# An eighth place for the experts' weights, and eight low parts of weights subtracted on GpSimd

## The chip, the cores and the metric

One core of a Trainium2 chip runs the whole program. The metric is the device time of one execution in microseconds; three runs of the kernel before gave 1318.97, 1319.60 and 1320.26 us (median 1319.6). Every time within an execution is counted from the first instruction of its profile.

## What is computed

Two transformer blocks in f32 over 256 tokens of width 1024. The first block ends in a mixture of experts; the second has a long convolution (Hyena), a differential attention and a gated feed-forward part. Cut to what the change touches:

```python
def hierarchical_moe(xn, w_rg, b_rg, w_re, b_re, w1, w3, w2):      # 4 groups of 8 experts, 2 experts for each token
    ...
    def block_ffn(args):
        tok, e = args
        xb = xt[tok]
        hb = jax.nn.silu(xb @ w1[e]) * (xb @ w3[e])                # w1, w3: 1024 x 512; w2: 512 x 1024
        return hb @ w2[e]
    ...
# first block: x += hybrid_mixer(...); x += memory_cross_attention(...); x += hierarchical_moe(...); rmsnorm(x, norm_f_g)
# second block: h = modulate(rmsnorm_2(x, g_mix_pre)); proj = h @ w_in     (columns: Hyena 3 x 512, q, k, v 512 each, gates 2048)
    y_hy = hyena_branch(proj[..., :OFF_Q], *hy_p) @ w_hy_up
    ...
    o = diff_attention(q, k_all, v_all, lam)                       # keys and values of x and of the context
    y_att = heads_out(o, subln_g, lam_init) @ w_att_up
    g_hy, g_att = split(sigmoid(proj[..., OFF_G:]))
    mixed = (g_hy * y_hy + g_att * y_att) @ w_out
    x = x + g1 * rmsnorm_2(mixed, g_mix_post)
    f = swiglu(modulate(rmsnorm_2(x, g_ffn_pre), sh2, sc2), w_gate, w_up, w_down)
    x = x + g2 * rmsnorm_2(f, g_ffn_post)
```

All 32 experts are read whatever the routing, 201 MB of weights.

## The kernel before

It is written in raw instructions for each engine, each with its own program and with semaphores between them. There is no planner: the order in the text is the order on the engine.

**Weights outside the experts.** `ring` holds six slots of 16 KB a partition (2 MB each). SyncE loads units of 2 MB into five of them in the order of `units`, each when the unit that held the slot has been read (`load`, line 2750). The sixth slot (index R) and the slots that fall free hold high parts. Products there are made of three fp32r terms: a quarter of a unit is rounded to a high part by ScalarE (`split_high`, L2164), the rest of it is subtracted into the slot itself as its low part (`low = src - high`), by VectorE (`split_low`, L1337), and for quarters 4 to 23 by GpSimd (`POOL_LOWS`, L2679). TensorE waits for each quarter's parts (`quarter_high`, `quarter_low`) and multiplies in `three_terms` (L531).

**Experts.** Sixteen pairs of experts, six units a pair in the order w1, w3 of the first, w1, w3 of the second, w2 of both. The units go round `PLACES = R + 2 = 7` places: place 0 to 4 are ring slots, place 5 is the sixth slot, place 6 lies in `flank` (its rows 2 and 3, and `actT` behind them). SyncE loads unit i (`expert_load`, L2757) when unit i - 7 has been read: `computed` waits for `upped` (a w1 and w3 pair multiplied) or `down` (both w2 multiplied). The first seven loads wait in `set_free`. The last two w2 units go in eight pieces (L2788). In a pair TensorE does `up` (L924, L925), `scatter` of the pair before (L971), `up` again, `gather` (L901) for the next pair and `down` (L942; for the last pair `down_by_pieces`, L957). Behind the experts SyncE loads p4x, p5x, p0 and p1, in this order, each when the last unit in its place has been read (`last_of`); then TensorE multiplies p4x, p5x (for the context), p0, p1, p2, p4 and so on.

**Rows.** `rows` (4 x 1024, the same on all partitions) holds, while the experts run, g1 * g_mix_post in row 1 and g2's row in row 0. Behind `upped` 32 GpSimd loads row 2 (norm_f_g, L2728) and row 3 (hy_bias, L2729).

**Attention of the second block.** Eight steps n. TensorE: scores of n + 1 (L1132), one quarter of p7 (steps 0 to 3) or p8 (4 to 7) as filler (L531), transposed weights (L1139), weighted values (L1146). The fillers' outputs use banks 6 and 7. VectorE: maxima of n + 1 (L1992) and their scaling (L1993), one low part (L1337), `differ` (L1998 to L2000), output (L2006). ScalarE: exponentials (L2525), one high part (L2164), after step 3 the emptying of banks 6 and 7 (`gate_columns`, L2514), then the transposed weights (L2539).

Of the kernel before, what the change touches and what calls it, by code (L numbers as in the profile page):

```python
# [24 lines left out]
P = 128  # L25
# [107 lines left out]
def two_blocks(nc, w, out):  # L133
# [18 lines left out]
    with ExitStack() as ctx:  # L152
# [15 lines left out]
        arena, arena_parts = both("arena", [P, 16384])  # L168
        flank, flank_parts = both("flank", [P, 4 * D + KD * N])
        rows = flank[:, 0:4 * D].rearrange("p (r n) -> p r n", r=4)  # L170
        actT, actT_parts = [f[:, 4 * D:4 * D + KD * N].rearrange("p (k n) -> p k n", k=KD) for f in (flank, flank_parts)]
        ident = sb("ident", [P, P])
        ones = sb("ones", [P, P])
        before = sb("before", [P, P])
        upto = sb("upto", [P, P])
        late = sb("late", [P, P])
        slots = sb("slots", [P, C])
        eps = sb("eps", [P, 1])
        sheet = sb("sheet", [P, P])
        cols1 = sb("cols1", [P, S1_ROWS])  # L180
        gmoe = sb("gmoe", [P, KD])
        cols2 = sb("cols2", [P, S2_ROWS])
        stat = sb("stat", [P, 64])
        msq = sb("msq", [P, 24, 2])
        work = sb("work", [P, 768])
        wif = sb("wif", [P, KD, 32])
        wroute = sb("wroute", [P, KD, NG + NE])
        rbias = sb("rbias", [P, NG + NE])
        bif = sb("bif", [H, 2])
        adaT = sb("adaT", [P, 32, 2])  # L190
        scT = sb("scT", [P, KD, 32])
        pick = sb("pick", [P, 2 * H])
        gsc = sb("gsc", [P, 3, KD])
        rope = sb("rope", [P, 2, NT, 64])
        count_i = sb("count_i", [1, 1], I32)
        lam = sb("lam", [P, 4, 64])
        subg = sb("subg", [P, DV])
# [135 lines left out]
        bank_full = [sem(f"bank_full{b}") for b in range(8)]  # L333
        POOL_LOWS = range(4, 24)
        part_read = sem("part_read")
        high_ready, low_ready = sem("high_ready"), sem("low_ready")
# [9 lines left out]
        for name in ("E_ready G_ready O_rms On_ready SVn_ready Y_ready Z_ready a_ready choice_ready "  # L346
                     "comb2_ready comb_ready consts count_ready if_zeros gmoe_in ctx_in decay_cols dexp dmax down filt_arg "
                     "filt_in squared hid_ones fw3_in filt_sin gate_rows hF_ready h_rms if_ready lam_dot lam_exp lam_in mem_in "
                     "misc_in norm_hat norm_rms out_stored p_ready qk_ready order_ready pick_ready G2_ready O_ms O_clamped rope_done rope_in "
                     "route_exp route_in rows1_in rows2_in rowf_in rows_g rowsh_in rowsp_in sheet1_in sheet2_in silu_c "  # L350
                     "gut_silu dft_in v_ones pool_low upped wroute_in x0_in x1_in x_new xexp xmax ").split():
            s[name] = sem(name)

        PLACES = R + 2

# [15 lines left out]
        def moe_place(m):  # L371

            if m == PLACES - 1:
                return flank[:, 2 * D:2 * D + 4096]
            return ring[:, R if m == R else (N_BEFORE + FREED[m]) % R, :]

        def moe_unit(n, u):
# [79 lines left out]
        def _(pe):  # L457
# [41 lines left out]
            def quarter_low(name, q):  # L499
                n = quarter_at(name, q)  # L500
                if n in POOL_LOWS:
                    pe.wait_ge(s["pool_low"], n - POOL_LOWS[0] + 1)
                else:
                    pe.wait_ge(low_ready, n + 1 if n < POOL_LOWS[0] else n + 1 - len(POOL_LOWS))

# [441 lines left out]
            def down_by_pieces(n):  # L947

                w2u = [moe_place((WHOLE + j) % PLACES).rearrange("p (k n) -> p k n", k=KF) for j in range(2)]
                reach(pe, moe["hid"], 2 * n + 2)  # L950
                for half in range(2):
                    reach(pe, moe[f"low{half}"], n)
                for k in range(KF):
                    pe.wait_ge(last_piece[k], 32)
                    for half in range(2):
                        for j in range(2):
                            mm = pe.matmul(PS[4 + half][j * C:(j + 1) * C, :], hidT[:, j, k, :],  # L957
                                           w2u[j][:, k, half * 512:(half + 1) * 512], start=(k == 0), stop=(k == KF - 1),
                                           skip_group_check=True)
                        if k == KF - 1:  # L960
                            mm.then_inc(moe["down"], 1)
# [361 lines left out]
        def _(dve):  # L1323
# [3 lines left out]
            def split_low(count=4):  # L1327

                for _ in range(count):
                    n = lows[0]  # L1330
                    lows[0] += 1
                    if lows[0] == POOL_LOWS[0]:
                        lows[0] += len(POOL_LOWS)
                    if n < len(SPLIT):
                        src, low, high = quarter(n)
                        dve.wait_ge(high_ready, n + 1)
                        dve.tensor_tensor(low, src, high, ALU.subtract).then_inc(low_ready, 1)  # L1337
# [605 lines left out]
            split_low(2)  # L1943
            dve.wait_ge(s["rowsh_in"], 16)

            def filtered(o):
# [687 lines left out]
        def _(pool):  # L2634
# [40 lines left out]

            for n in POOL_LOWS:
                src, low, high = quarter(n)
                pool.wait_ge(high_ready, n + 1)
                pool.tensor_tensor(low, src, high, ALU.subtract).then_inc(s["pool_low"], 1)  # L2679

            for h in range(H):
# [44 lines left out]

            pool.wait_ge(moe["upped"], 2 * PAIRS)
            pool.dma_start(rows[:, 2, :], w["norm_f_g"].rearrange("(a n) -> a n", a=1).broadcast_to([P, D])).then_inc(s["rowf_in"], 16)  # L2728
            pool.dma_start(rows[:, 3, :], w["hy_bias_2"].rearrange("a o n -> a (o n)").broadcast_to([P, D])).then_inc(s["rowsh_in"], 16)  # L2729

            pool.wait_ge(s["Z_ready"], 4)
            pool.dma_start(rows[:, 3, :], w["g_ffn_post_2"].broadcast_to([P, D])).then_inc(s["rowsh_in"], 16)


        @block.sync
        def _(sp):
# [29 lines left out]
            def set_free(m):  # L2766

                if m == PLACES - 1:
                    full(sp, "logits")
                    sp.wait_ge(s["rows_g"], 1)  # L2770
                elif m == R:
# [6 lines left out]
            for i, (n, u) in enumerate(order):  # L2778
                if i < PLACES:
                    set_free(i)  # L2780
                else:
                    computed(*order[i - PLACES])
                if i < WHOLE:
                    expert_load(i % PLACES, 2 * n + u // 3, u % 3)
            for k in range(KF):
                for j in range(2):
                    src = w["w2"][0, NE - 2 + j].rearrange("(p k) n -> p k n", p=P)
                    sp.dma_start(moe_place((WHOLE + j) % PLACES)[:, k * D:(k + 1) * D], src[:, k, :]).then_inc(last_piece[k], 16)  # L2788
            sp.wait_ge(s["count_ready"], 1)
# [11 lines left out]
            for i in range(N_BEFORE, N_BEFORE + R - 1):  # L2801
                computed(*max(order[j] for j in range(len(order)) if j % PLACES == last_of[AT[i]]))
                load(i)
# [59 lines left out]
```

## Time and profile before

| | |
|---|---|
| median of three runs | 1319.6 us |
| the profiled execution | 1319.89 us, span 1318.1 us, mean granted clock of TensorE 0.998 |
| TensorE busy | 1279.4 us (97%) in 7078 matmuls |
| VectorE, ScalarE, GpSimd busy | 699.9, 500.4, 77.7 us |
| DMA | 363.67 MB, mean 276 GB/s; SyncE's queue 69.1% of 16 engines' span |
| experts' products, L924 and L925 | 432 and 448 matmuls (and 80 and 64 from `flank`), 598 ns each |
| low parts on VectorE, L1337 | 214, 1223 ns each |
| low parts on GpSimd, L2679 | 20, 2446 ns each |

A line number is that of the kernel. PE is TensorE's multiplication and PEld its weight load, DVE VectorE, ACT ScalarE, POOL GpSimd, SP SyncE; a `q` behind a name is that engine's queue. In the lines of the timeline the first number is the start and the second the duration, in us; brackets give how long the engine stood idle before and what ended that. "issue" is time in which the engine waited for nothing that the profile shows, and waits of TensorE for a load of the experts' weights appear so.

### The profile page before, as it was taken

What the parts mean: (1) busy time and instruction counts of PE and PEld (TensorE: products, weight loads), DVE (VectorE), ACT (ScalarE), POOL (GpSimd) and SP (SyncE); (2) the same over time, 40 slices, a digit from 0 to 9 for tenths busy, and PEclk for the clock granted to TensorE, in tenths of its full rate; (3) what the DMA queues carried; (4) which work ended last, traced back from release to release, by engine and by line L of the source; (5) the groups of instructions that cost most, each with busy time, mean ns of one, the idle gap of its engine ahead of it and who ended that gap; (6) DMA issues with size and microseconds to landing.
All of it is one profiled execution on the core that took longest, in us unless ns stands there. A gap on an engine that the chain in (4) does not pass through costs nothing.

```text
span 1318.1 us, 17839 instructions
## 1 busy us (share of the span) xinstructions
PE 1279.4 (97%) x7078; PEld 891.5 (68%) x7078; DVE 699.9 (53%) x1198; ACT 500.4 (38%) x766; POOL 77.7 (6%) x86
## 2 busy tenths in 40 slices
PE   8999999999999999999999999999999999999998
PEld 7987886976675454444454444459956687799986
DVE  5665678667564322223222222257875878755552
ACT  5556574344332111111111111156414585744442
POOL 6730200100000000000000000000000000000000
PEclk9999999999999999999999999999999999999999
DMA  9644648949855999999999999995505335655540
GB/s 352 239 180 164 227 144 299 348 178 340 309 202 222 403 429 426 426 429 428 427 427 427 428 426 429 423 385 175 192 1 206 129 136 158 194 164 180 191 160 33
DMA packets 102212, 363.67 MB, mean 276 GB/s; under 512 B 4098, under 2 KB 28933, under 8 KB 90032
## 3 DMA queue, kind: packets, MB, share of 16 engines
q1 hardware_dynamic: 98656, 352.86, 69.1%
q0 software_dynamic: 3280, 9.58, 2.2%
q8 instruction: 59, 0.97, 0.3%
q14 instruction: 25, 0.20, 0.0%
q10 hardware_dynamic: 192, 0.06, 0.0%
HBM read 361.43 MB, written 1.05 MB: 275 GB/s over the span
## 4 chain that ended last, share of the span: by engine, by line
PE 84%; DVE 8%; ACT 4%; issue 2%; DMA 1%; ACTq 0%; DVEq 0%
PE bank L531 37%; PE bank L924 17%; PE bank L942 8%; PE bank L901 5%; PE bank L1289 5%; PE bank L971 3%; DVE ring_parts L1337 2%; PE bank L932 1%; PE bank L1092 1%; ACT ring_parts L2164 1%; PE bank L585 1%; DMA ring<-in_w_xkv 1%; PE bank L620 1%; PE bank L853 1%; PE bank L925 1%
## 5 line engine op out<-in xcount | busy, mean ns | idle before, releaser
L2164 ACT ACTIVATE ring_parts<-ring 128x1024 fp32r<-128x1024 f32 x234 | 242.6, 1057 | 227.8 <-PE bank L531 200.3
L1337 DVE TENSOR_TENSOR ring_parts<-ring,ring_parts 128x1024 fp32r<-128x1024 f32 x214 | 257.1, 1223 | 131.1 <-ACT ring_parts L2164 128.4
L531 PE MATMUL bank<-ring_parts,arena_parts 128*128 128x512 f32 x1056 | 271.8, 392 | 3.6 <-ACT ring_parts L2164 1.5
L531 PEld LDWEIGHTS bank<-ring_parts,arena_parts 128*128 128x128 f32 x1056 | 196.5, 188 | 48.9 <-ACT ring_parts L2164 2.9
L531 PE MATMUL bank<-arena_parts,ring_parts 128*128 128x256 f32 x1504 | 198.0, 284 | 2.8 <-DVE ring_parts L1337 1.6
L924 PE MATMUL bank<-ring,arena 128*64 128x512 f32 x432 | 192.3, 598 | 7.9 <-issue 7.9
L925 PE MATMUL bank<-ring,arena 128*64 128x512 f32 x448 | 199.6, 599 | 0.0
L531 PEld LDWEIGHTS bank<-arena_parts,ring_parts 128*128 128x128 f32 x1504 | 190.1, 192 | 4.9 <-issue 3.1
L924 PEld LDWEIGHTS bank<-ring,arena 128*64 128x64 f32 x432 | 57.8, 138 | 128.3 <-issue 128.1
L531 PE MATMUL bank<-ring_parts 128*128 128x512 f32 (+1 forms) x624 | 117.1, 346 | 2.1 <-DVE ring_parts L1337 1.2
L531 PEld LDWEIGHTS bank<-ring_parts 128*128 128x128 f32 x624 | 96.6, 190 | 22.1 <-issue 7.9
L2418 ACT ACTIVATE arena<-bank 128x512 f32<-128x512 f32 x32 | 19.1, 598 | 229.6 <-PE bank L925 229.6
L942 PE MATMUL bank<-ring,arena 128*64 128x512 f32 x416 | 106.3, 595 | 0.0
L1840 DVE TENSOR_TENSOR x<-x,bank 128x512 f32<-128x512 f32 x64 | 41.1, 684 | 109.8 <-PE bank L971 109.7
L1811 DVE TENSOR_TENSOR arena<-bank,gmoe 128x512 f32<-128x512 f32 x32 | 22.1, 692 | 108.2 <-PE bank L901 108.2
L1831 DVE SCALAR_TENSOR_TENSOR arena_parts<-bank,stat,arena_parts 128x512 fp32r<-128x512 f32 x32 | 24.0, 751 | 101.7 <-ACT arena_parts L2431 101.6
L531 PE MATMUL bank<-ring_parts,flank_parts 128*128 128x512 f32 x192 | 69.8, 391 | 0.1
L942 PEld LDWEIGHTS bank<-ring,arena 128*64 128x64 f32 x416 | 32.7, 137 | 53.5 <-issue 52.0
L2431 ACT ACTIVATE arena_parts<-bank,stat 128x512 fp32r<-128x512 f32 x32 | 22.0, 687 | 123.1 <-PE bank L942 116.2
L901 PEld LDWEIGHTS bank<-arena 128*128 128x128 f32 x512 | 59.6, 192 | 12.7 <-issue 12.7
L901 PE MATMUL bank<-arena 128*128 128x128 f32 x512 | 63.8, 278 | 0.0
L1289 PE MATMUL bank<-ring_parts,arena_parts 128*128 128x512 f32 x264 | 60.0, 389 | 0.0
(391 smaller groups left out, 1419.6 us busy)
## 6 DMA issues: line engine op xcount, KB each, us to landing
ring<-in_w SPq DMA_DIRECT2D x81, 2048.0 KB, 21.5
ring<-in_w_in SPq DMA_DIRECT2D x27, 2048.0 KB, 9.8
flank<-in_w SPq DMA_DIRECT2D x13, 2048.0 KB, 22.2
ring<-in_w_ada SPq DMA_DIRECT2D x12, 2048.0 KB, 8.6
ring<-in_w_ffn_gate SPq DMA_DIRECT2D x11, 1024.0 KB, 5.4
ring<-in_w_ffn_up SPq DMA_DIRECT2D x11, 1024.0 KB, 8.0
ring<-in_w_ffn_down SPq DMA_DIRECT2D x5, 2048.0 KB, 7.7
ring<-in_w_xkv SPq DMA_DIRECT2D x4, 2048.0 KB, 16.6
```

The source lines that it names most:

```text
L531: mm = pe.matmul(ps[:, o:o + width], *pair, start=(o == 0 and kk == 0 and ha + hw == 0), stop=(kk == kn - 1 and (ha, hw) == terms[-1] and ...
L901: mm = pe.matmul(PS[half][:, k * P:(k + 1) * P], hat3[:, t, (4 * half + k) * P:(4 * half + k + 1) * P], selB[:, t, :], start=(t == 0), sto ...
L924: pe.matmul(PS[2][0:C, :], xgT[:, k, j, :], w1u[:, k, :], start=(k == 0), stop=(k == KD - 1))
L925: mm = pe.matmul(PS[2][C:2 * C, :], xgT[:, k, j, :], w3u[:, k, :], start=(k == 0), stop=(k == KD - 1))
L942: mm = pe.matmul(PS[4 + half][j * C:(j + 1) * C, :], hidT[:, j, k, :], w2u[j][:, k, half * 512:(half + 1) * 512], start=(k == 0), stop=(k ...
L971: mm = pe.matmul(PS[6 + t][:, :], selT[:, t * P:(t + 1) * P], yB[part][:, half * 512:(half + 1) * 512], start=(part == 0), stop=(part == 1))
L1289: mm = pe.matmul(accs[t][half][:], act_f[:, t * P:(t + 1) * P], wts[:, 0, half * 512:(half + 1) * 512], start=(f == 0 and n == 0), stop=(f ...
L1337: dve.tensor_tensor(low, src, high, ALU.subtract).then_inc(low_ready, 1)
L1811: dve.tensor_tensor(xgT[:, 4 * half:4 * half + 4].rearrange("p k b c -> p k (b c)"), PS[half][:].rearrange("p (k c) -> p k c", k=KD // 2), ...
L1831: dve.scalar_tensor_tensor(out=yB[1][:, c], in0=PS[4 + half][:], scalar=slot_gate, in1=yB[0][:, c], op0=ALU.mult, op1=ALU.subtract).then_i ...
L1840: dve.tensor_tensor(xs, xs, PS[6 + t][:], ALU.add).then_inc(moe["acc"], 1)
L2164: act.activation(high, src, ACT.Copy).then_inc(high_ready, 1)
```

## The change

The number of places becomes eight. `flank` grows to hold two whole places: place 6 is its first 16 KB (all four rows), place 7 the next (`actT`, and tiles that are dead by then, which move into it: `work`, `scT`, `wif`, `lam`, `late`, `sheet`, `cols1`, `wroute`). Rows 0 and 1 are therefore stored to DRAM by GpSimd before place 6 is loaded, and read back, broadcast to all partitions, once hy0_0 (the first output bank of p0) is full. The load of norm_f_g moves ahead to `upped` 30, that of hy_bias behind hy0_0. The last two w2 units take places 0 and 1 (`place_of`). The low parts of p7 and p8 (the gate columns under the attention, four quarters each) are subtracted by GpSimd behind its last DMA; VectorE passes over them.

```diff
+        TAIL = 4 * D + KD * N
+        flank, flank_parts = both("flank", [P, TAIL + 768 + 3 * 256 + 2 * P + S1_ROWS + KD * (NG + NE)])
+        work = flank[:, TAIL:TAIL + 768]
...
+        row_stash = nc.dram_tensor("row_stash", (2, D), F32, kind="Internal").ap()
...
+        POOL_LATE = ("p7", "p8")
...
-        PLACES = R + 2
+        PLACES = R + 3
...
-            if m == PLACES - 1:
-                return flank[:, 2 * D:2 * D + 4096]
+            if m > R:
+                return flank[:, 4096 * (m - R - 1):4096 * (m - R)]
             return ring[:, R if m == R else (N_BEFORE + FREED[m]) % R, :]
+
+        def place_of(i):
+            return (i if i < WHOLE else i - UNITS) % PLACES
...
             def quarter_low(name, q):
                 n = quarter_at(name, q)
+                late = sum(entry[0] in POOL_LATE for entry in SPLIT[:n + 1])
                 if n in POOL_LOWS:
                     pe.wait_ge(s["pool_low"], n - POOL_LOWS[0] + 1)
+                elif name in POOL_LATE:
+                    pe.wait_ge(s["pool_low"], len(POOL_LOWS) + late)
                 else:
-                    pe.wait_ge(low_ready, n + 1 if n < POOL_LOWS[0] else n + 1 - len(POOL_LOWS))
+                    pe.wait_ge(low_ready, n + 1 if n < POOL_LOWS[0] else n + 1 - len(POOL_LOWS) - late)
...
-                    if n < len(SPLIT):
+                    if n < len(SPLIT) and SPLIT[n][0] not in POOL_LATE:
                         src, low, high = quarter(n)
...
             dve.wait_ge(s["rowsh_in"], 16)
+            dve.wait_ge(s["rows_back"], 16 * 2)
...
-            pool.wait_ge(moe["upped"], 2 * PAIRS)
+            pool.wait_ge(s["rows_g"], 1)
+            for i in range(2):
+                pool.dma_start(row_stash[i:i + 1, :], rows[0:1, i, :]).then_inc(s["rows_kept"], 16)
+
+            pool.wait_ge(moe["upped"], 2 * (PAIRS - 1))
             pool.dma_start(rows[:, 2, :], w["norm_f_g"].rearrange("(a n) -> a n", a=1).broadcast_to([P, D])).then_inc(s["rowf_in"], 16)
+            full(pool, "hy0_0")
+            for i in range(2):
+                pool.dma_start(rows[:, i, :], row_stash[i:i + 1, :].broadcast_to([P, D])).then_inc(s["rows_back"], 16)
             pool.dma_start(rows[:, 3, :], w["hy_bias_2"].rearrange("a o n -> a (o n)").broadcast_to([P, D])).then_inc(s["rowsh_in"], 16)

             pool.wait_ge(s["Z_ready"], 4)
             pool.dma_start(rows[:, 3, :], w["g_ffn_post_2"].broadcast_to([P, D])).then_inc(s["rowsh_in"], 16)
+            for n, entry in enumerate(SPLIT):
+                if entry[0] in POOL_LATE:
+                    low_part(n)
...
-                if m == PLACES - 1:
+                if m == R + 1:
                     full(sp, "logits")
-                    sp.wait_ge(s["rows_g"], 1)
+                    sp.wait_ge(s["rows_kept"], 16 * 2)
+                elif m == R + 2:
+                    full(sp, "logits")
...
-                    computed(*order[i - PLACES])
+                    computed(*order[max(j for j in range(i) if place_of(j) == place_of(i))])
...
-                    sp.dma_start(moe_place((WHOLE + j) % PLACES)[:, k * D:(k + 1) * D], src[:, k, :]).then_inc(last_piece[k], 16)
+                    sp.dma_start(moe_place(place_of(WHOLE + j))[:, k * D:(k + 1) * D], src[:, k, :]).then_inc(last_piece[k], 16)
...
             for i in range(N_BEFORE, N_BEFORE + R - 1):
-                computed(*max(order[j] for j in range(len(order)) if j % PLACES == last_of[AT[i]]))
+                computed(*max(order[j] for j in range(len(order)) if place_of(j) == last_of[AT[i]]))
                 load(i)
```

`low_part(n)` is the body of the old loop over `POOL_LOWS`: wait for the high part, subtract, signal `pool_low`.

## Rows read from the trace of the kernel before

**Rows 1.** Windows view: stretch, PE, PEld, DVE, ACT, POOL busy; PEclk, DMA share, GB/s.

```profile
411.00:424.00 13.00, 13.00 (x71) 6.62 (x69) 5.14 (x25) 1.08 (x2) 0.00 (x0) 1.00 0.01 4
446.00:848.00 402.00, 392.41 (x2040) 181.10 (x2036) 110.95 (x266) 51.21 (x112) 0.00 (x0) 1.00 1.01 427
```

**Rows 2.** Chain that ended last, through the experts: start us, us, what.

```profile
437.78 7.02 PE bank L942 x32
465.65 7.02 PE bank L942 x32
...
729.14 2.53 issue
740.46 1.12 PE bank L971 x4
...
847.87 1.26 issue
856.21 1.13 PE bank L971 x4
```

**Rows 3.** Waits view, 440 to 880 us: total, times, longest.

```profile
PE bank L924 <- issue: 10.7, 8, 2.5
```

**Rows 4.** SyncE's queue at the end of the experts: start us, us, issue.

```profile
856.25 0.38 SPq L2750 DMA_DIRECT2D ring<-in_w_in  x1
```

**Rows 5.** DMA view, three issues (856, 926, 890 us): KB, us to landing.

```profile
ring<-in_w_in SPq DMA_DIRECT2D x1, 2048.0 KB, 21.4
...
ring<-in_w_in SPq DMA_DIRECT2D x1, 2048.0 KB, 7.7
...
ring<-in_w_in SPq DMA_DIRECT2D x1, 2048.0 KB, 8.5
```

**Rows 6.** Timeline, end of the experts and the product behind them.

```profile
875.47 0.69 ACT L2431 ACTIVATE arena_parts<-bank,stat 128x512 fp32r<-128x512 f32 x1 [0.17 <-PE bank L957]
...
877.69 2.96 ACT L2164 ACTIVATE ring_parts<-ring 128x1024 fp32r<-128x1024 f32 x3 [1.53 <-DMA ring<-in_w_in]
877.92 1.25 PE L971 MATMUL bank<-arena_parts 128*128 128x512 f32 x4 [0.42 <-DVE x L1840]
...
879.23 0.47 PE L531 MATMUL bank<-ring_parts,flank_parts 128*128 128x512 f32 x1
```

**Rows 7.** Page, GpSimd's DMA queue: packets, MB, share of 16 engines.

```profile
q0 software_dynamic: 3280, 9.58, 2.2%
```

**Rows 8.** Windows view after the longest wait (columns as in rows 1).

```profile
731.00:737.00 6.00, 5.33 (x18) 2.11 (x20) 0.00 (x0) 0.00 (x0) 0.00 (x0) 0.72 1.02 434
```

**Rows 9.** Timeline, VectorE beside GpSimd's subtractions, and one of those.

```profile
54.49 0.28 DVE L1436 TENSOR_SCALAR flank<-flank 4x256 f32<-4x256 f32 x1
...
66.55 2.31 DVE L1443 TENSOR_SCALAR flank<-flank 4x256 f32<-4x256 f32 x1
...
72.48 2.69 DVE L1421 SCALAR_TENSOR_TENSOR arena<-bank,cols,arena 128x255 f32<-128x255 f32 x6
...
61.02 2.41 POOL L2679 TENSOR_TENSOR ring_parts<-ring,ring_parts 128x1024 fp32r<-128x1024 f32 x1 [2.75 <-ACT ring_parts L2164]
```

**Rows 10.** Timeline, the attention of the second block.

```profile
1025.33 2.97 PE L531 MATMUL bank<-ring_parts 128*128 128x512 f32 x12 [1.16 <-DVE ring_parts L1337]
...
1025.76 1.06 ACT L2164 ACTIVATE ring_parts<-ring 128x1024 fp32r<-128x1024 f32 x1
...
1028.24 0.17 DVE L1993 TENSOR_SCALAR stat<-stat 128x2 f32<-128x2 f32 x1
...
1030.23 1.06 ACT L2164 ACTIVATE ring_parts<-ring 128x1024 fp32r<-128x1024 f32 x1
...
1033.10 0.17 DVE L1993 TENSOR_SCALAR stat<-stat 128x2 f32<-128x2 f32 x1
...
1040.30 1.13 PE L1132 MATMUL bank<-arena 64*128 64x512 f32 x4
...
1042.08 3.01 PE L531 MATMUL bank<-ring_parts 128*128 128x512 f32 x12 [0.65 <-ACT arena L2514]
```

More of the change, by code:

```diff
@@ L168, in two_blocks @@
         arena, arena_parts = both("arena", [P, 16384])
-        flank, flank_parts = both("flank", [P, 4 * D + KD * N])
+        TAIL = 4 * D + KD * N
+        flank, flank_parts = both("flank", [P, TAIL + 768 + 3 * 256 + 2 * P + S1_ROWS + KD * (NG + NE)])
         rows = flank[:, 0:4 * D].rearrange("p (r n) -> p r n", r=4)
         actT, actT_parts = [f[:, 4 * D:4 * D + KD * N].rearrange("p (k n) -> p k n", k=KD) for f in (flank, flank_parts)]
+        work = flank[:, TAIL:TAIL + 768]
+        scT, wif, lam = [flank[:, TAIL + o:TAIL + o + 256].rearrange("p (k c) -> p k c", k=k) for o, k in ((768, KD), (1024, KD), (1280, 4))]
+        late, sheet = [flank[:, TAIL + o:TAIL + o + P] for o in (1536, 1664)]
+        cols1 = flank[:, TAIL + 1792:TAIL + 1792 + S1_ROWS]
+        wroute = flank[:, TAIL + 1792 + S1_ROWS:].rearrange("p (k c) -> p k c", k=KD)
+        row_stash = nc.dram_tensor("row_stash", (2, D), F32, kind="Internal").ap()
         ident = sb("ident", [P, P])
@@ L175, in two_blocks @@
         upto = sb("upto", [P, P])
-        late = sb("late", [P, P])
         slots = sb("slots", [P, C])
         eps = sb("eps", [P, 1])
-        sheet = sb("sheet", [P, P])
-        cols1 = sb("cols1", [P, S1_ROWS])
         gmoe = sb("gmoe", [P, KD])
@@ L184, in two_blocks @@
         msq = sb("msq", [P, 24, 2])
-        work = sb("work", [P, 768])
-        wif = sb("wif", [P, KD, 32])
-        wroute = sb("wroute", [P, KD, NG + NE])
         rbias = sb("rbias", [P, NG + NE])
@@ L190, in two_blocks @@
         adaT = sb("adaT", [P, 32, 2])
-        scT = sb("scT", [P, KD, 32])
         pick = sb("pick", [P, 2 * H])
@@ L195, in two_blocks @@
         count_i = sb("count_i", [1, 1], I32)
-        lam = sb("lam", [P, 4, 64])
         subg = sb("subg", [P, DV])
@@ L349, in two_blocks @@
                      "misc_in norm_hat norm_rms out_stored p_ready qk_ready order_ready pick_ready G2_ready O_ms O_clamped rope_done rope_in "
-                     "route_exp route_in rows1_in rows2_in rowf_in rows_g rowsh_in rowsp_in sheet1_in sheet2_in silu_c "
+                     "route_exp route_in rows1_in rows2_in rowf_in rows_kept rows_back rows_g rowsh_in rowsp_in sheet1_in sheet2_in silu_c "
                      "gut_silu dft_in v_ones pool_low upped wroute_in x0_in x1_in x_new xexp xmax ").split():
             s[name] = sem(name)
-        PLACES = R + 2
+        PLACES = R + 3
         def moe_sems(tag):
@@ L947, in down_by_pieces @@
             def down_by_pieces(n):
-                w2u = [moe_place((WHOLE + j) % PLACES).rearrange("p (k n) -> p k n", k=KF) for j in range(2)]
+                w2u = [moe_place(place_of(WHOLE + j)).rearrange("p (k n) -> p k n", k=KF) for j in range(2)]
                 reach(pe, moe["hid"], 2 * n + 2)
@@ L2674, in _, with low_part @@
                 pool.dma_start(sheet[o:o + n, :], src).then_inc(s["sheet2_in"], 16)
-            for n in POOL_LOWS:
+            def low_part(n):
                 src, low, high = quarter(n)
@@ L2679, in _ @@
                 pool.tensor_tensor(low, src, high, ALU.subtract).then_inc(s["pool_low"], 1)
+            for n in POOL_LOWS:
+                low_part(n)
             for h in range(H):
@@ L2732, in _ @@
             pool.dma_start(rows[:, 3, :], w["g_ffn_post_2"].broadcast_to([P, D])).then_inc(s["rowsh_in"], 16)
+            for n, entry in enumerate(SPLIT):
+                if entry[0] in POOL_LATE:
+                    low_part(n)
         @block.sync
```

## The prediction

> **What bounds the kernel now.** I read the windows view first, then the chain of work that ended last, then the waits at its seams. TensorE is busy all through, so a change can pay only where TensorE waits. In the experts' stage (446 to 848 us) the DMA engines are at their full share for the whole 402 us, at 427 GB/s, while TensorE loses 402 - 392.4 = 9.6 us [rows 1]. The chain gives the same from the other side. A pair of experts costs TensorE 465.65 - 437.78 = 27.9 us; its six places of weights cost the DMA engines 6 x 2.097 MB / 427 GB/s = 29.5 us [rows 1, 2]. So once the early lead is used up, every pair waits at its first product (L924) for its weights: 10.7 us in eight waits, the longest 2.53 [rows 2, 3]. The last, of 1.26 us, ends at 849.13 [rows 2].
>
> Behind the experts the next product needs unit p4x. SyncE issues it at 856.25, as soon as `upped` reaches 31, but the experts' last weights are ahead of it in the queue, and it lands 21.4 us later, at 877.65 [rows 4, 5]. ScalarE's first pass over it starts at 877.69, TensorE's product at 879.23, just behind the last scatter (877.92) [rows 6]. So TensorE waits for nothing there. In the attention the steps are TensorE's, with two waits: 1.16 us for a low part from VectorE, 0.65 us for ScalarE's emptied bank [rows 10].
>
> **1. The eighth place.** Its load goes out behind the seventh's at about 403 us; the DMA engines move nothing from 411 to 424 us [rows 1], so the extra 2 MB is free, and so is a stash of two rows of 4 KB that lands late by a few us: that place is first read in the second pair. From then on each place is freed at the same moments as before, so every unit is one transfer ahead: 2.097 / 427 GB/s = 4.9 us earlier at the end of the stage. Against it: the row load of norm_f_g (512 KB) moves from behind the experts to `upped` 30, in front of the last pair's weights. At 427 GB/s it costs 1.2 us; by GpSimd's queue as a whole (2.2% of 1318 us for 9.58 MB) 1.6 [rows 7]. I take 1.4. Net, the experts end 3.5 us earlier (bounds 3.3 and 4.9). 3.5 is less than the 10.7 us of waits, so the stage stays with the DMA engines.
>
> **2. What the eighth place does to p4x.** `place_of` puts the last pair's two w2 units into places 0 and 1, which are the ring slots that p4x and p5x take next. The last user of place 0 was unit 91, so p4x waited for `upped` 31. It is now unit 94, so SyncE waits for `down` 32, the end of the last down product, with p5x, p0 and p1 queued behind. That end is now at about 875.4, where ScalarE takes the second bank [rows 6]; 3.5 earlier it is 871.9. By then the engines have nothing left: p4x pays issue to landing alone. Such a load takes 7.7 us at 926 and 8.5 at 890 [rows 5]; I take 8.1. Landing: 880.0, against 877.65. In the kernel before TensorE took its product some 0.5 us after ScalarE's first pass (877.69 + 1.0) had allowed it, so of the 2.4 us later landing **+1.9** reaches TensorE. Bounds: +0.1 (the full 4.9, 7.7) to +2.5 (3.3, 8.5). The gain of part 1 is spent in this sum. The later units follow 5 us apart and are read 11 us apart: no further wait. The norm of x hangs on ScalarE behind the same passes and moves with them.
>
> The Trainium skill (DMA: Bandwidth & Descriptors, Anatomy of one DMA) puts a transfer's fixed part at about 2.0 us beside its bytes. The row of 7.7 us less 4.9 of bytes is 2.8. By the page the landing would be 1.2 us sooner and the step +0.7; the row decides.
>
> **3. TensorE's clock behind that wait.** TensorE is done with the scatter at 879.2 - 3.5 = 875.7 and starts p4x at 881.1: 5.4 us idle. Behind the idle 2.53 us at 729.14 the granted clock was 0.72 over 731 to 737 [rows 8], that is, part of it at 1.2 GHz instead of 2.4, and the product up to the next scatter took 740.46 - 731.67 = 8.79 us, against 856.21 - 849.13 = 7.08 behind the 1.26 us wait [rows 2]: 1.7 us. I charge the same, **+1.7**; bounds 0 and 3.4 (twice as long at the lower clock).
>
> **4. The rows that come back.** 3 x 512 KB from GpSimd once hy0_0 is full. Three whole products (p1, p2, p4) lie between that and VectorE's wait for them, against 8 us or so for a landing [rows 5]: 0. GpSimd itself waits there with only the late low parts behind it. Adding a wait to VectorE costs nothing while the loads are that early; without that cover it would be one landing, some 8 us.
>
> **5. Eight low parts on GpSimd.** VectorE is rid of eight subtractions; of these only one stood on the path, the 1.16 us wait [rows 10]. That gain does not last. From there to 1042.08 the chain is VectorE's maxima, ScalarE's exponentials, VectorE's mixing, 1033.10 - 1028.24 = 4.86 us a step, and the subtraction lay beside the exponentials. TensorE, sooner by 1.16 us, waits at 1042.08 for ScalarE's emptied bank instead [rows 10].
>
> GpSimd takes 2.41 us for one such part [rows 9]. In time it is early enough: the high part is ready at 1026.8 [rows 10], the low one at 1029.3, and the product that reads it is the next step's, behind the scores. The point is what it does to VectorE. Where GpSimd subtracted early in the kernel, a VectorE tensor_scalar from SBUF to SBUF that takes 0.28 us alone took 2.31, and ended with GpSimd's instruction; operations with an input in PSUM kept their 0.45 (six in 2.69) [rows 9]. Each step has one of the hurt kind on its chain, L1993, between maxima and exponentials. GpSimd would run behind ScalarE's pass: 1026.82 to 1029.28, and L1993 is due at 1028.24: 1.04 late. In the next step 1031.34 to 1033.75, due at 1033.10: 0.65 late; the third the same [rows 9, 10]. ScalarE empties the bank 2.35 us later: **+2.4** at 1042.08. Bounds: -1.2 (nobody is hurt and the gain lasts) and +7.2 (a whole GpSimd instruction in each of three steps). Behind that TensorE's steps (5.4 us) are longer than the chain's, and nothing is added. The idle time at 1042.08 grows from 0.65 to between 3.0 and 4.2 us, again more than the 2.53 us that brought the clock down: **+1.7**, bounds 0 and 3.4.
>
> The Trainium skill (GPSIMD Engine Reference, Key points) says that GpSimd shares its SBUF interfaces with VectorE, and contends with VectorE instructions in a 2-port mode or with two SBUF inputs. The rows agree for a tensor_scalar of 256 elements; that the rule holds for the 2 elements of L1993 no row shows. If it didn't, the sum would lose 2.4 + 1.7.
>
> **Sum.** Profiled execution 1319.89 us (span 1318.1 and 1.8 around it); the median of the runs is 0.3 below it. 1319.9 + 1.9 + 1.7 + 2.4 + 1.7 = 1327.6, less 0.3 for the median: **1327.3**.
>
> **Rivals.**
> - All of it, and the clock falls in the last pair too: its wait was 1.26 us, and the row load in front of it makes it 2.5 to 2.9, about the size that did it once. 1.7 more: 1329.0.
> - GpSimd hurts nobody: L1993 is too short. 1319.6 + 1.9 + 1.7 = 1323.2. For it: no row with so small an operation beside GpSimd. Against: L1443, whose cost was not its own length but waiting.
> - The clock stays up at both places, since one row is all that speaks for the fall (the chain shows waits up to 1.5 us without it): 1319.6 + 1.9 + 2.4 = 1323.9.
> - Faster: the lead is kept. That needs p4x landed by 878 or so less the 3.5: 874 to 875, within 3 us of the issue, or an issue before the last down product's end. It decides at an issue-to-landing time of 5.7 us (871.9 + 5.7 = 877.6); shorter than that, part of the 3.5 stays, at most all: 1316.1. Against: 7.7 is the least of a lone 2 MB in rows 5.
> - The change does little: the full 4.9, a landing of 7.7, no fall and no contention: 1319.7. It would say that the parts are done but every price is at its lower bound.
>
> **How the numbers follow.** Forecast 0.38; all three falls of the clock 0.17; GpSimd hurts nobody 0.20; clock stays up 0.12; little 0.08; faster 0.05. A measurement of this kernel tells 0.2% (2.6 us) from no change, so "slower" begins at 1322.2. The first two are slower; of the next two most (their bounds reach under 1322.2): 0.83. Same 0.12, faster 0.05. The range leaves out the faster case and the least of the "little", and twice the clock's price above: 1320.8 to 1330.8.
>
> **What the profile would show.** Part 1: waits at L924 of about 7 us in all instead of 10.7, the last w2 product some 3.5 us earlier. Part 2: SyncE's issue of p4x only at the last down product's end, DMA engines idle for some 6 us before it, a landing about 8 us later, TensorE idle 5 us. Part 3: a granted clock under 1 behind it. Part 5: L1993 of 0.8 to 1.2 us instead of 0.17 in the first steps, GpSimd's instructions ending with it, TensorE's wait for the bank at 3 us or more. I am wrong if p4x is issued before that end, if L1993 keeps 0.17, or if the idle times leave the clock at 1.

## The result, and the profile after

The changed kernel takes 1329.4 us (median of 4 runs, 1327.0 to 1331.0) against 1319.9 (1319.0 to 1320.3): 1.0063 times the kernel before, 95% interval 1.0044 to 1.0082, slower by 8 us by that ratio and by 9.5 by the two medians. The forecast was 1327.3 us, slower. The profiled execution took 1330.8 us, its span 1329.1, against 1318.1 before: 11.0 us more. All readings here are of that execution, and it is at the upper end of its runs.

The page of the changed kernel: span, and the granted clock in 40 slices.

```profile
span 1329.1 us, 17843 instructions
...
PEclk9999999999999999999999999989999999999999
```

The windows view of the changed kernel (columns as in rows 1): the experts' stage; the last pair's wait; the product p4x behind the experts; the attention behind the bank wait.

```profile
446.00:848.00 402.00, 394.44 (x2054) 181.06 (x2052) 112.07 (x267) 52.48 (x113) 0.56 (x1) 1.00 1.01 427
847.00:853.00 6.00, 6.00 (x22) 2.23 (x23) 0.00 (x0) 0.00 (x0) 0.00 (x0) 0.72 1.00 423
882.00:888.00 6.00, 2.85 (x7) 2.32 (x8) 2.96 (x3) 4.03 (x6) 0.00 (x0) 0.50 1.04 383
1052.00:1056.00 4.00, 4.00 (x13) 3.02 (x12) 2.07 (x5) 2.62 (x5) 1.01 (x2) 0.57 0.22 89
```

The DMA engines still run the experts' stage at 427 GB/s, and TensorE now loses 7.6 us there instead of 9.6 [rows 1]. What is new is the last column but two: a granted clock of 0.72, 0.50 and 0.57 at three places where it was 1. The fall in the middle of the stage is there as before: 2.53 us of waiting at 729.14 then, 2.74 at 725.45 now.

The chain of work that ended last, changed kernel: start us, us, what.

```profile
844.36 2.54 issue
...
867.76 7.11 PE bank L963 x32
...
874.89 9.04 DMA ring<-in_w_in
...
883.95 1.06 ACT ring_parts L2171
...
885.15 12.84 PE bank L537 x48
```

The chain now runs through a transfer. In the kernel before it went from the scatter at 877.92 straight into the product at 879.23, and p4x had been issued at 856.25 [rows 4, 6]. Now p4x is issued at 874.89, in the moment in which the last down product ends, and lands 9.04 us later. The waits view says how long TensorE stood (us in total, times, longest):

```profile
PE bank L930 <- issue: 7.6, 4, 2.7
PE bank L537 <- ACT ring_parts L2171: 6.6, 1, 6.6
```

L930 is L924 of before: 7.6 us in 4 waits, where rows 3 had 10.7 in 8. The 6.6 us are p4x's.

The timeline of the changed kernel in the attention, GpSimd, VectorE and TensorE (start us, us, engine, line, operation):

```profile
1034.46 2.35 POOL L2686 TENSOR_TENSOR ring_parts<-ring,ring_parts 128x1024 fp32r<-128x1024 f32 x1 [9.02 <-ACT ring_parts L2171]
1039.80 2.37 POOL L2686 TENSOR_TENSOR ring_parts<-ring,ring_parts 128x1024 fp32r<-128x1024 f32 x1 [2.99 <-ACT ring_parts L2171]
...
1035.87 0.97 DVE L2000 TENSOR_SCALAR stat<-stat 128x2 f32<-128x2 f32 x1
...
1041.60 0.60 DVE L2000 TENSOR_SCALAR stat<-stat 128x2 f32<-128x2 f32 x1
...
1051.56 4.58 PE L537 MATMUL bank<-ring_parts 128*128 128x512 f32 x12 [3.21 <-ACT arena L2521]
```

GpSimd's subtraction ends at 1034.46 + 2.35 = 1036.81; the tensor_scalar of two elements (L2000, before L1993 with 0.17 us) starts at 1035.87, takes 0.97 and ends at 1036.84. The next pair: 1042.17 and 1042.20. TensorE then waits 3.21 us for the bank that it waited 0.65 for [rows 10], and its product takes 4.58 us instead of 3.01.

One part of the 11.0 us lies ahead of everything that was changed. The chain of the kernel before, and then that of the changed one, in the first block:

```profile
213.56 9.92 DMA ring<-in_w_xkv
...
226.04 11.74 PE bank L531 x96
```

```profile
213.62 10.07 DMA ring<-in_w_xkv
...
226.24 13.25 PE bank L537 x96
```

The same 96 products behind the same wait took 11.74 us and 13.25. The clock granted over 226 to 232 us was 1.00 before and 0.72 in the changed kernel. Of the ten profiles of the experiments below, all with this stretch as here, only e4's shows the fall too, so it belongs to the execution, not to the change. It is 1.7 us by GpSimd's iota, which stands just in front of the experts (395.09 and 396.80), and it may be why this execution is 1.4 us over its median: only one of the four was profiled.

Two more rows of the kernel before's chain, for the ledger: the 48 products of p4x, and the attention's first tensor_scalar.

```profile
879.23 11.17 PE bank L531 x48
...
1019.20 0.18 DVE stat L1993
```

The attention's stretch is taken from there to the product behind the bank wait: 1042.08 - 1019.20 = 22.88 us before, 1051.56 - 1026.77 = 24.79 after. The ledger, changed kernel less kernel before, from these rows:

| stretch | us |
|---|---|
| first block, clock | +1.7 |
| to the last scatter (877.92 to 877.34, less the 1.7) | -2.3, of it clock in the last pair +1.7 |
| wait for p4x: 885.15 - 878.58, against 0.06 | +6.5 |
| p4x's product, clock: 12.84 - 11.17 | +1.7 |
| attention: 24.79 - 22.88 | +1.9 |
| that product, clock: 4.58 - 3.01 | +1.6 |
| sum | 11.1 |

### The profile page after: what moved, and what is told of

It reads as the page before. It is cut to its first block, busy times and chain, and to the rows that moved or that the text cites. A ratio compares the mean times of both kernels' runs of the same rounds, so it can differ in the third digit from the quotient of the medians.

```text
span 1329.1 us, 17843 instructions
## 1 busy us (share of the span) xinstructions
PE 1284.7 (97%) x7078; PEld 893.6 (67%) x7078; DVE 692.2 (52%) x1190; ACT 500.7 (38%) x766; POOL 98.7 (7%) x98
## 4 chain that ended last, share of the span: by engine, by line
PE 84%; DVE 8%; ACT 4%; issue 2%; DMA 1%; ACTq 0%; DVEq 0%
PE bank L537 37%; PE bank L930 17%; PE bank L948 8%; PE bank L907 5%; PE bank L1295 5%; PE bank L977 2%; DVE ring_parts L1343 2%; PE bank L938 1%; PE bank L1098 1%; ACT ring_parts L2171 1%; PE bank L591 1%; DMA ring<-in_w_xkv 1%; PE bank L626 1%; PE bank L859 1%; DMA ring<-in_w_in 1%
## 5 line engine op out<-in xcount | busy, mean ns | idle before, releaser
L1343 DVE TENSOR_TENSOR ring_parts<-ring,ring_parts 128x1024 fp32r<-128x1024 f32 x206 | 247.3, 1223 | 138.2 <-ACT ring_parts L2171 135.8
L930 PE MATMUL bank<-ring,arena 128*64 128x512 f32 x384 | 172.8, 604 | 6.5 <-issue 6.5
L931 PE MATMUL bank<-ring,arena 128*64 128x512 f32 x384 | 173.0, 604 | 0.0
L930 PEld LDWEIGHTS bank<-ring,arena 128*64 128x64 f32 x384 | 51.9, 139 | 115.4 <-issue 115.3
L948 PE MATMUL bank<-ring,arena 128*64 128x512 f32 x384 | 85.0, 595 | 0.0
L2686 POOL TENSOR_TENSOR ring_parts<-ring,ring_parts 128x1024 fp32r<-128x1024 f32 x28 | 67.4, 2420 | 49.8 <-ACT ring_parts L2171 49.8
```

What stands on the lines that cost most here:

```text
L930: pe.matmul(PS[2][0:C, :], xgT[:, k, j, :], w1u[:, k, :], start=(k == 0), stop=(k == KD - 1))
L931: mm = pe.matmul(PS[2][C:2 * C, :], xgT[:, k, j, :], w3u[:, k, :], start=(k == 0), stop=(k == KD - 1))
```

## The experiments

All ratios are to the kernel before, run beside them on the same chip, with 95% intervals; the median of the kernel before was 1320.2 us beside e1 to e4, 1320.8 beside e5 to e8 and 1322.1 beside e9 and e10.

**Which half of the change costs what: e1 and e2.** e1 is the changed kernel with

```
-POOL_LATE = ("p7", "p8")
+POOL_LATE = ()
```

> The changed kernel with all low parts of p7 and p8 back on VectorE; the eighth place and what comes with it stay. My theory: the attention is as in the kernel before (a wait of 1.2 us and one of 0.65 us, the clock up there), and what is left of the loss is p4x: the experts end 3.1 us earlier than in the kernel before plus 1.7 us where the clock falls in the last pair, p4x's product starts 2.5 us later than before without that fall, and its first half runs at the lower clock, 1.7 us. 1319.9 + 2.5 + 1.7 + 1.7 = 1325.8 us, 1324.1 without the fall in the last pair. Rival, the low parts are not to blame (the later start of the attention alone shifts its waits): the time stays at the changed kernel's 1329.4 us, and the waits in the attention stay at 3 us.

Measured: 1325.9 us (1322.7 to 1328.5), 1.0043 (1.0028 to 1.0058). Its chain and, in the timeline, its attention:

```profile
842.25 2.98 issue
...
873.21 9.33 DMA ring<-in_w_in
...
883.77 12.80 PE bank L537 x48
```

```profile
1048.21 3.00 PE L537 MATMUL bank<-ring_parts 128*128 128x512 f32 x12 [0.65 <-ACT arena L2521]
```

The attention is that of the kernel before to the hundredth (22.88 us from its first L2000 to the product behind the bank wait, wait 0.65). p4x is as late as in the changed kernel.

e2 is the kernel before with the eight low parts on GpSimd and nothing else (the hunks of the diff that name POOL_LATE).

> The kernel before with the eight low parts of p7 and p8 on GpSimd and nothing else of the change. My theory: the 1.16 us wait goes, the tensor_scalar of 2 elements between maxima and exponentials takes 0.6 to 1 us in three or four steps, TensorE waits about 3 us for the emptied bank and its clock falls behind that: +1.9 + 1.6 = 1323.4 us. Rival, the contention belongs to the later start of the attention in the changed kernel, or is covered here: 1318.7 to 1319.9 us, and that operation keeps 0.17 us.

Measured: 1323.6 us (1322.7 to 1326.4), 1.0027 (1.0018 to 1.0037). Timeline:

```profile
1026.12 2.35 POOL L2683 TENSOR_TENSOR ring_parts<-ring,ring_parts 128x1024 fp32r<-128x1024 f32 x1 [8.91 <-ACT ring_parts L2168]
...
1027.53 0.97 DVE L1997 TENSOR_SCALAR stat<-stat 128x2 f32<-128x2 f32 x1
...
1043.22 5.46 PE L535 MATMUL bank<-ring_parts 128*128 128x512 f32 x12 [3.21 <-ACT arena L2518]
```

The same 0.97 us, the same 3.21, and 24.80 us for the stretch: the loss is the GpSimd parts' own and does not hang on the later start. The clock's part is larger here, 5.46 - 3.01 = 2.5 us, in this one execution. The two halves add up within their intervals: 0.43% and 0.27%, 0.70% in all, against 0.63%.

**Is it the slot that makes p4x late: e3.** One number, which gives p4x and p5x the slots of the places that units 90 and 91 free at `upped` 31:

```
-    turns = [0]
+    turns = [2]
```

> The changed kernel, but the units behind the experts take the ring's slots in turns that start two further on: p4x and p5x go where units 90 and 91 were (free at upped 31), p0 and p1 where the last two w2 units are. My theory (p4x is late because its slot is freed last): it is issued at upped 31, lands by about 875 us, TensorE goes from the scatter into its product without a wait and at the full clock, the 3.1 us lead is kept: 1319.9 - 3.1 + 1.7 (clock in the last pair) + 3.5 (attention) = 1322.0 us, 1320.3 without the fall in the last pair. Rival (the queue behind the last experts' weights, or the row load, is what makes p4x late, not its slot): it lands at 880 or later and the time stays at 1327 to 1329.4 us.

Measured: 1322.3 us (1317.8 to 1325.0), 1.0015 (1.0005 to 1.0026). Timeline, SyncE and TensorE:

```profile
854.20 20.17 SPq L2770 DMA_DIRECT2D ring<-in_w_in  x4
...
875.82 1.24 PE L977 MATMUL bank<-arena_parts 128*128 128x512 f32 x4 [0.41 <-DVE x L1846]
877.09 0.47 PE L537 MATMUL bank<-ring_parts,flank_parts 128*128 128x512 f32 x1
...
1041.77 3.01 PE L537 MATMUL bank<-ring_parts 128*128 128x512 f32 x12 [3.21 <-ACT arena L2521]
```

p4x is issued at 854.20, and TensorE goes from the scatter into its product with no wait and 0.47 us for the first product, the full clock. The slot it was. Some 6 us of the changed kernel's loss (1.0063 against 1.0015) hang on which of two places is freed first. The last row is of the attention: the same 3.21 us wait as in the changed kernel, and here the product behind it took 3.01 us: the clock did not fall. So a wait of that length brings it down in some executions (two of three profiles), not in all. This execution, of 1319.5 us, is the second fastest of e3's eleven: the median is 2.8 us higher. Its mean granted clock was 0.998, that of the other ten 0.994 to 0.997, so its 3.01 us are not the usual case.

**All three mended: e4.** `turns = [2]`, POOL_LATE empty, and the row load behind `upped` 32 again:

```
-            pool.wait_ge(moe["upped"], 2 * (PAIRS - 1))
+            pool.wait_ge(moe["upped"], 2 * PAIRS)
```

> The eighth place with three things mended: slots in turns that start two further on, all low parts of p7 and p8 on VectorE, and the row load of norm_f_g again behind upped 32. My theory: the whole lead of one transfer, 4.9 us, reaches the end, and no wait is long enough to bring the clock down behind it: 1319.9 - 4.9 = 1315.0 us (1314 to 1317). Rival (a lead in the experts is worth nothing, since what stands behind them is bound by transfers or by ScalarE's passes): 1318.5 to 1320.5 us.

Measured: 1316.2 us (1315.0 to 1317.9), 0.9969 (0.9957 to 0.9980): faster than both kernels. Timeline, TensorE:

```profile
845.85 0.61 PE L930 MATMUL bank<-ring,arena 128*64 128x512 f32 x1 [1.25 <-issue]
...
874.65 1.24 PE L977 MATMUL bank<-arena_parts 128*128 128x512 f32 x4 [0.41 <-DVE x L1846]
875.97 0.47 PE L537 MATMUL bank<-ring_parts,flank_parts 128*128 128x512 f32 x1
```

From the iota to the last scatter 874.65 - 396.79 = 477.9 us, against 482.8 before: 5.0 earlier, one transfer. The last pair's wait is 1.25 us.

**What the clock costs behind the wait: e5.** As e1, with this ahead of p4x's first product:

```
+            for _ in range(50):
+                pe.transpose(PS[JOB[p4c[0][0]][0]][:, 0:P], ident[:], ident[:])
```

> The eighth place with the low parts back on VectorE (as in e1), and 50 transposes of 128 x 128, 0.117 us each by the profile's L606 (5.9 us), in the wait for p4x, which is about 6.9 us. They compute nothing that is used. My theory: TensorE's clock stays up behind that wait, where it fell in e1, and the product's first half takes 1.7 us less: e1's 1325.9 - 1.7 = 1324.2 us; waits elsewhere keep their clock. Rival (the slower product is not the clock's doing, or the transposes come in the way of it): 1325.9 us or more.

Measured: 1324.7 us (1322.4 to 1329.4), 1.0027 (1.0014 to 1.0040). Timeline and chain:

```profile
877.18 5.65 PE L1036 MATMUL bank<-ident 128*128 128x128 f32 x50
884.10 0.50 PE L537 MATMUL bank<-ring_parts,flank_parts 128*128 128x512 f32 x1 [1.27 <-ACT ring_parts L2173]
```

```profile
873.65 9.31 DMA ring<-in_w_in
...
884.10 11.20 PE bank L537 x48
```

The load takes as long as in e1 (9.31 and 9.33 us), but the 48 products behind it take 11.20 us, as in the kernel before (11.17), instead of 12.80. The clock itself, by the windows view of e1 and then of e5 (columns as in rows 1):

```profile
884.00:888.00 4.00, 4.00 (x11) 3.12 (x12) 3.15 (x3) 3.97 (x6) 0.00 (x0) 0.59 1.05 388
```

```profile
882.00:886.00 4.00, 2.73 (x16) 2.19 (x15) 1.92 (x2) 3.01 (x4) 0.00 (x0) 1.00 1.05 387
```

The clock's price is 1.6 us; the clock, not the data, made them slow. The executions that were not profiled agree: the median of the mean granted clock is 0.998 in e5's twelve and 0.995 in e1's seven. By ratio the step is 1.0043 - 1.0027, 2.1 us, with intervals that overlap.

**What the row load costs: e6.** As e1, with e4's third edit.

> As e1 (eighth place, low parts on VectorE, p4x in the slot freed last), but the row load of norm_f_g again behind upped 32 instead of in front of the last pair's weights. My theory: the last pair's wait at its first product falls from 3.0 us to about 1.25 and the clock stays up there; the experts end 1.7 + 1.7 us earlier, p4x is issued and lands as much earlier, 8 to 9 us after its issue: 1325.9 - 3.4 = 1322.5 us. Rival (the row load does not delay the weights by more than its 1.2 us of bytes, and the clock falls anyway): 1324.7 us; if it costs nothing at all, 1325.9.

Measured: 1324.6 us (1321.9 to 1328.4), 1.0026 (1.0014 to 1.0039). Timeline and chain:

```profile
842.66 0.61 PE L930 MATMUL bank<-ring,arena 128*64 128x512 f32 x1 [1.27 <-issue]
```

```profile
868.98 9.53 DMA ring<-in_w_in
...
879.74 12.94 PE bank L537 x48
```

The last pair's wait is 1.27 us with a product at the full clock, where e1 had 2.98 and a fall. From the iota to the last scatter it is 3.2 us less than in e1 (477.3 and 480.5), near the 3.4 expected: 1.7 of clock and 1.5 for the row load. But this is the fastest of e6's twelve executions. The median, 1324.6, is the rival's figure and not my 1322.5, and by the ratios the step is 2.2 us, with intervals that overlap. So the trace shows what the row load costs in one execution, and the usual execution gains less; e10, which also loads the row late, shows a way in which some lose it again (below).

**Does the contention need the overlap: e7 and e8.** e7 is the kernel before with each of the eight low parts cut in two: GpSimd columns 0 to 511, VectorE 512 to 1023.

> The kernel before with the low parts of p7 and p8 cut in two: GpSimd takes 512 of the 1024 columns (1.2 us instead of 2.36), VectorE the other 512. My theory (what costs in e2 is that GpSimd's instruction is still running when the 128 x 2 tensor_scalar is due, 1.8 us after the high part): the GpSimd instruction ends before that, the tensor_scalar keeps 0.17 us, and the loss is gone; the 1.16 us wait shrinks by half or so and comes back at the emptied bank: 1319.3 to 1320.2 us. Rival (any GpSimd work in the attention costs, or the low part comes too late from GpSimd): 1322 to 1323.5 us, as e2.

Measured: 1321.2 us (1319.1 to 1322.7), 0.9995 (0.9984 to 1.0006). Timeline:

```profile
1027.86 1.28 POOL L2684 TENSOR_TENSOR ring_parts<-ring,ring_parts 128x512 fp32r<-128x512 f32 x1 [10.71 <-ACT ring_parts L2169]
...
1029.20 0.17 DVE L1998 TENSOR_SCALAR stat<-stat 128x2 f32<-128x2 f32 x1
...
1025.77 2.99 PE L536 MATMUL bank<-ring_parts 128*128 128x512 f32 x12 [0.63 <-DVE ring_parts L1342]
...
1043.04 3.00 PE L536 MATMUL bank<-ring_parts 128*128 128x512 f32 x12 [1.20 <-ACT arena L2519]
```

GpSimd is done at 1029.14, before 1029.20, and the tensor_scalar keeps its 0.17. The waits are 0.63 and 1.20 us in place of 1.16 and 0.65: what the shorter subtraction saves at the first comes back at the second, and the stretch is 22.87 us, as before.

In e8, the whole low parts are on GpSimd as in e2, but four of them wait for the step's tensor_scalar:

```
+                if j in (2, 3, 4, 5):
+                    pool.wait_ge(s["dmax"], j + 1)
                 low_part(n)
```

> As e2 (the kernel before, low parts of p7 and p8 on GpSimd), but four of them start only when VectorE has done the step's 128 x 2 tensor_scalar, 1.5 us later than in e2. My theory (a short VectorE instruction from SBUF to SBUF waits for the end of GpSimd's): the tensor_scalar keeps 0.17 us in those steps, and the reciprocal 1.9 us behind it takes 0.6 to 0.8 us instead of 0.17; the time stays at e2's 1323.5 us, within 1. Rival (the low parts' lateness costs, not the contention): the later start adds 1.5 us in each of two steps or more: 1326 us or more, with TensorE waiting for GpSimd's low part.

Measured: 1321.8 us (1319.5 to 1325.6), 1.0009 (0.9996 to 1.0022). Timeline:

```profile
1030.66 2.34 POOL L2683 TENSOR_TENSOR ring_parts<-ring,ring_parts 128x1024 fp32r<-128x1024 f32 x1 [10.54 <-DVE stat L1997]
...
1032.39 0.17 DVE L2002 RECIPROCAL stat<-stat 128x2 f32<-128x2 f32 x1 [1.81 <-ACT flank L2529]
1032.59 0.43 DVE L2003 SCALAR_TENSOR_TENSOR stat<-stat 128x1 f32<-128x1 f32 x1
...
1033.15 2.99 PE L535 MATMUL bank<-ring_parts 128*128 128x512 f32 x12 [1.02 <-POOL ring_parts L2683]
...
1044.82 3.00 PE L535 MATMUL bank<-ring_parts 128*128 128x512 f32 x12 [0.97 <-ACT arena L2518]
```

Neither side had it right. The tensor_scalar kept 0.17 us, as I said, but the reciprocal, which starts in the middle of GpSimd's instruction, kept its 0.17 too; it is the scalar_tensor_tensor behind it that was held, 0.43 us for 0.22, until GpSimd's end at 1033.00. So little is left to hold, and the stretch takes 23.50 us, 0.6 over that of before and 1.3 under e2's. The lateness that the rival spoke of is there (1.02 us for GpSimd's part), once, and it takes the place of the kernel before's 1.16. It is not what costs in e2. From the iota to p4x's product this execution takes 3.3 us more than the kernel before (487.4 and 484.1), ahead of all the low parts that moved: the last pair waits 2.76 us instead of 1.26, and the clock falls there (0.75 over 848 to 854).

**Why p4x takes 9 us: e9.** As e6, and SyncE issues p5x only when p4x has landed:

```
                 load(i)
+                if i == N_BEFORE:
+                    sp.wait_ge(unit_loaded[AT[i]], 16 * PARTS_UP_TO[i])
```

> As e6 (eighth place, low parts on VectorE, row load late), but SyncE issues p5x only once p4x has landed, instead of p4x, p5x, p0 and p1 at once. In e6 p4x took 9.5 us from issue to landing, against 7.7 and 8.5 in the rows on which the forecast rested, where one load was issued alone or in a pair. My theory (the loads issued right behind it take a share of the DMA engines): p4x lands after 7.7 to 8.1 us, its product starts 1.4 to 1.8 us earlier, p5x lands some 8 us later and is still in time, 11 us behind p4x's start: 1324.6 - 1.5 = 1323.1 us. Rival (p4x takes 9.5 us because the engines had nothing to do before it, or because of what it reads): 9.3 us or more, and 1324.6 us; if p5x then comes too late, more.

Measured: 1324.5 us (1321.8 to 1326.8), 1.0019 (1.0009 to 1.0029). Chain:

```profile
870.46 7.67 DMA ring<-in_w_in
...
879.36 13.12 PE bank L537 x48
```

7.67 us from issue to landing, where the four profiles with the loads issued at once have 9.04, 9.33, 9.31 and 9.53. From the scatter's start to p4x's product it is 6.44 us against 8.31 in e6, 1.9 less. So the landing is my theory's, in one profile; the time is not: 1324.5 us is the rival's figure, and by ratio the step is 0.9 us, within the intervals. Both traces, e6's and this one's, are of the fastest of twelve executions.

**The gain once more, on another chip: e10.** As e4, but with e7's halves.

> As e4 (eighth place, slots in turns that start two further on, row load late), but the low parts of p7 and p8 are shared: 512 columns on GpSimd, 512 on VectorE, as in e7. My theory: the halves neither cost nor bring anything, the attention takes what it takes in e4, and the lead of the eighth place reaches the end: a ratio to the kernel before of 0.9969, as e4 (0.9955 to 0.998). Rival (e4's gain was its chip's or its runs'): 0.999 or more; rival (VectorE, freed of half its low parts, gains in the attention on top): 0.996 or less, with less waiting than 1.8 us in all there.

Measured: 1316.4 us (1314.4 to 1317.7), 0.9951 (0.9935 to 0.9968). Timeline, TensorE:

```profile
845.88 1.08 PE L931 MATMUL bank<-ring,arena 128*64 128x512 f32 x1 [2.76 <-issue]
...
1040.05 3.00 PE L538 MATMUL bank<-ring_parts 128*128 128x512 f32 x12 [1.22 <-ACT arena L2522]
```

The gain of the lead stands on a second chip. The ratio lies under the 0.9955 that I gave as the least, where the second rival had it, but the interval overlaps e4's, and the attention takes 22.88 us with 1.85 us of waits, as in the kernel before (22.88 and 1.81): the trace shows nothing that the halves bring. The first row has a wait of 2.76 us in the last pair and a first product of 1.08 us, with no row load in front. One wait that is 1 to 1.5 us longer than its neighbours appears in most profiles (before at 729, e4 at 755, e8 at 669); in the last pair no later wait for weights is left that could shrink by as much. Of the eight profiles whose row load is late it did so in two; of the four whose row load comes first, all have 2.5 to 3.0 us there and a fall. What the longer wait comes from is not shown.

## Why the prediction was right, point by point

**Part 1, the eighth place** (experts 3.5 us earlier, 3.3 to 4.9). Measured in the changed kernel: the last scatter 2.3 us earlier with 1.7 us of clock in it, so 4.0 us. The full lead without the row load is 5.0 us in e4 and 5.6 in e6, against 4.9 worked out; the row load is 1.5 us by e6 and e1 and 1.0 by e4 and the changed kernel (5.0 less 4.0), against 1.4.

**Part 2, p4x** (+1.9 net, +0.1 to +2.5). The issue waits for the end of the last down product, as forecast, and e3 shows that this alone costs. Net it was -4.0 + 6.5 = +2.5, at the upper bound. Two terms were off and partly cancel: the lead was 0.5 better, and issue to landing was 9.04 us, not 8.1. The rows that I took (7.7 and 8.5) were of loads with none or one behind them in the queue, and this one had three; e9 gives the 7.67 back. With the lead at its forecast size the sum would have gone over the upper bound. The Trainium skill (DMA: Bandwidth & Descriptors, Anatomy of one DMA) gives a fixed part of about 2.0 us, in a section on transfers that GpSimd issues, while these are SyncE's. The measured landings less 4.9 of bytes leave 2.8 for the held load and 4.1 to 4.6 for the others, so none of these loads agrees with it.

**Part 3, the clock behind it** (+1.7, 0 to 3.4). 1.7 in the chain, 1.6 by e5. The clock was low for longer than behind the wait that I took the price from, but part of that time lay over the wait itself and cost nothing: in e1 it is 0.56 over 880 to 884 us, where TensorE stands idle until 883.77, 0.59 over 884 to 888 and 1.00 over 888 to 892.

**Part 4, the rows that come back** (0). GpSimd issues them at 921.0 to 922.1, the last lands 7.3 us later, and VectorE comes to its wait for them at 965.8, behind its two low parts; the next operation there is released by TensorE. No run of its own tested it.

**Part 5, the low parts** (+2.4 and +1.7; -1.2 to +7.2). Place and mechanism were as forecast: L1993 held to the end of GpSimd's instruction, 0.80, 0.43 and 0.48 us late in the first three steps for the forecast 1.04, 0.65 and 0.65, since L1993 ends together with GpSimd's instruction, where I had let it start (0.17 less), and that instruction took 2.35 us, not 2.41. The stretch grew by 1.9, and the fall of the clock behind it added 1.6. That the 1.16 us gain does not last is shown by e7. The doubt that I kept open, whether so small an operation can be held, is settled by e1 and e2. The Trainium skill (GPSIMD Engine Reference, Key points) names VectorE instructions in a 2-port mode or with two SBUF inputs. e8 agrees with it more closely than my own theory: the reciprocal, with one input, ran untouched beside GpSimd, and the scalar_tensor_tensor, with two, was held. The tensor_scalar has one input too and was held; that it ran in a 2-port mode no run shows.

**The sum.** The forecast's terms come to 7.7 (-3.5 and +5.4, which are its +1.9, then 1.7, 2.4 and 1.7); the same ones measure -4.0 + 6.5 + 1.7 + 1.9 + 1.6 = 7.7. What is on top in the profiled execution are the two falls of the clock that the forecast left out: in the last pair, which was its first rival (1329.0, chance 0.17) and which is what happened, and in the first block, which it had no row for. The median of 1329.4 is the rival's figure, but that it fits to 0.4 us is in part luck: the four executions are two of 1331 us (mean granted clock 0.991 and 0.992) and two of 1327 to 1328 (0.995 and 0.996), and none lies at the median. I gave the rival too little: the row load makes that wait 2.5 to 3.0 us, where I had written 2.5 to 2.9, and the clock fell in four profiles of four.

**The other rivals.** GpSimd hurts nobody: refuted (e2). The clock stays up: refuted for p4x (four profiles with a wait of 5.2 to 7.1 us, four falls, and none in e5), open by execution for the bank wait (two of three). The lead is kept: not in this kernel, and true as soon as the slot is changed (e3, e4, e10).

What stays open is what the single longer wait in the experts' stage comes from, why the clock fell in the first block in two profiles, and why a load with others behind it takes 1.4 to 1.9 us longer.

## What to carry to other kernels

A deeper buffer pays only if what stands behind the loop can start from a slot that is freed early: before adding a place, list for each of the first units behind it which event now frees its slot, and give the first unit the slot that is freed first. A small load put in front of the last weights costs its bytes, and as much again in clock where the wait that it lengthens lets TensorE's clock fall, as the waits of 2.5 to 3.0 us did here. Work moved to GpSimd beside a chain on VectorE should end before the chain's next instruction of a kind that is held (here tensor_scalar and scalar_tensor_tensor, not reciprocal); half the columns did, all of them did not.

## What the runs showed of the hardware that I had not expected

- Beside a GpSimd tensor_tensor of 128 x 1024, VectorE's reciprocal of 128 x 2 kept 0.17 us, while a tensor_scalar of 128 x 2 (0.17 us) took up to 0.97 and a scalar_tensor_tensor of 128 x 1 (0.22 us) 0.43, both ending with GpSimd's instruction (e2, e8).
- A 2 MB load took 9.0 to 9.5 us with three issued right behind it from the same engine (four profiles) and 7.67 when the next was held back (one, e9).
- Behind waits of 2.3 to 3.2 us TensorE's granted clock fell in most cases and not in others: it fell behind 2.30 us in e2 (0.57 over 731 to 735 us) and behind 2.53 in the kernel before (0.72 over 731 to 737), and stayed at 1.00 behind 2.72 us in e8 (672 to 676) and behind 3.21 in e3 (1044 to 1048). Behind 5.2 us and more it fell in each of four profiles (in the changed kernel 0.50, which is 1.2 GHz, over the whole of 882 to 888 us). A fall cost 1.5 to 2.0 us, and 2.5 in e2's attention.
